# Expert weights in a ring of four 4 MB slots instead of six 2 MB slots, in a one-core decoder-layer kernel

## What is computed

```python
def moe_ffn(u, w_router, b_router, w_gate, b_gate, w_up, b_up, w_down, b_down):
    logits = (xf @ w_router + b_router).astype(F32)
    top_val, top_idx = lax.top_k(logits, TOP_K)
    gates = jax.nn.softmax(top_val, axis=-1)
    ...
        gt = jnp.minimum(xblk @ w_gate[e] + b_gate[e], SWIGLU_LIMIT)
        up = jnp.clip(xblk @ w_up[e] + b_up[e], -SWIGLU_LIMIT, SWIGLU_LIMIT)
        hdn = (up + 1.0) * gt * jax.nn.sigmoid(gt * SWIGLU_ALPHA)
        return hdn @ w_down[e] + b_down[e]
```

## Time and profile before

| | |
|---|---|
| runs | 1271.01, 1271.86, 1273.28 us, median 1271.86 |
| span of the profiled execution | 1267.4 us |
| profiled execution's own time beside its span | not listed apart from the runs; its span is 4.5 us under their median |
| busy | PE 1174.1 us, DVE 487.1 us, ACT 195.6 us, POOL 4.6 us |
| moved by DMA | 451.37 MB |

### The profile page before, as it was taken

One profiled execution on the slowest core, in us unless ns is written; L12 is line 12 of the kernel. 1 busy time (PEld: TensorE's weight loads), 2 busy tenths in 40 slices (PEclk: granted clock), 3 DMA queues, 4 the chain that ended last, 5 costly groups with the idle time before them and its releaser, 6 DMA issues.

```text
span 1267.4 us, 21244 instructions
## 1 busy us (share of the span) xinstructions
PE 1174.1 (93%) x8502; PEld 557.1 (44%) x8503; DVE 487.1 (38%) x1082; ACT 195.6 (15%) x431; POOL 4.6 (0%) x28
## 2 busy tenths in 40 slices
PE   8999989999998989999899999799999888879896
PEld 7888768874333333333333433233433333232333
DVE  2799998115342322232312233222232332323233
ACT  2143504022111100111101111100111110110112
POOL 0000000000000000000000000000000000000000
PEclk9999999999999999999989999999999999998998
DMA  9551329615999999899999899998999999999995
GB/s 395 208 186 67 142 105 330 268 53 209 411 428 425 427 429 400 329 430 427 428 430 402 342 430 428 428 428 353 392 430 430 429 427 429 428 430 428 428 429 228
DMA packets 36997, 451.37 MB, mean 356 GB/s; under 512 B 5112, under 2 KB 5656, under 8 KB 10080
## 3 DMA queue, kind: packets, MB, share of 16 engines
q1 hardware_dynamic: 35344, 449.02, 85.1%
q10 hardware_dynamic: 1616, 1.82, 0.4%
HBM read 443.57 MB, written 7.25 MB: 356 GB/s over the span
## 4 chain that ended last, share of the span: by engine, by line
PE 58%; DMA 28%; DVE 12%; issue 1%; DVEq 1%; ACT 0%; POOL 0%; SPq 0%; POOLq 0%; ACTq 0%
DMA ring<-in_w_experts 27%; PE ps L1467 25%; PE ps L1510 9%; DVE acts L724 5%; PE ps L1244 3%; PE ps L1346 3%; PE ps L1444 3%; PE ps L1519 2%; PE ps L1403 2%; PE ps L1477 2%; PE ps L1218 2%; DVE acts L819 1%; PE ps L1457 1%; PE ps L1337 1%; PE ps L1500 1%
## 5 line engine op out<-in xcount | busy, mean ns | idle before, releaser
L1467 PE MATMUL ps<-ring,extra 128*64 128x512 f32 x1824 | 424.1, 610 | 12.4 <-DMA ring<-in_w_experts 12.4
L1077 DVE TENSOR_TENSOR acts<-ps,acts 128x528 f32<-128x528 f32 x128 | 90.6, 708 | 403.0 <-PE ps L1477 201.6
L1467 PEld LDWEIGHTS ps<-ring,extra 128*64 128x64 f32 x1824 | 124.2, 139 | 265.5 <-issue 237.5
L1510 PE MATMUL ps<-ring,extra 128*32 128x256 f32 x3072 | 201.7, 398 | 38.3 <-DMA ring<-in_w_experts 34.8
L1510 PEld LDWEIGHTS ps<-ring,extra 128*32 128x32 f32 x3072 | 89.7, 113 | 140.0 <-DMA ring<-in_w_experts 50.9
L724 DVE SCALAR_TENSOR_TENSOR acts<-acts,small 128x256 f32<-128x256 f32 x224 | 91.3, 477 | 0.7 <-ACT acts L453 0.7
L1244 PE MATMUL ps<-acts,ring 128*128 128x280 f32 (+1 forms) x320 | 75.3, 394 | 0.3 <-ACT ring L524 0.3
L1244 PEld LDWEIGHTS ps<-acts,ring 128*128 128x128 f32 x320 | 60.5, 190 | 14.2 <-issue 1.0
L1244 PE MATMUL ps<-acts,extra 128*128 128x280 f32 x256 | 63.1, 409 | 1.9 <-DVE acts L706 1.9
L1091 DVE TENSOR_SCALAR extra<-ps 128x512 f32<-128x512 f32 x32 | 22.0, 689 | 96.3 <-PE ps L1467 81.0
L604 ACT ACTIVATE extra<-extra 128x512 f32<-128x512 f32 x32 | 19.7, 630 | 240.2 <-DVE extra L1082 240.2
(11 more groups left out here) (294 smaller groups left out, 898.9 us busy)
## 6 DMA issues: line engine op xcount, KB each, us to landing
ring<-in_w_experts SPq DMA_DIRECT2D x192, 2048.0 KB, 21.7
ring<-in_w_in_t SPq DMA_DIRECT2D x5, 2048.0 KB, 20.7
extra<-in_w_in_t SPq DMA_DIRECT2D x4, 2048.0 KB, 11.2
extra<-in_w_out_t SPq DMA_DIRECT2D x4, 1024.0 KB, 5.8
ring<-in_w_out_t SPq DMA_DIRECT2D x4, 1024.0 KB, 5.9
ring<-in_state_t SPq DMA_DIRECT2D x8, 512.0 KB, 6.9
ring<-dtx_rows SPq DMA_DIRECT2D x8, 512.0 KB, 5.8
out_ssm_s_t<-ring SPq DMA_DIRECT2D x8, 512.0 KB, 4.7
```

What stands on the lines that cost most here:

```text
L1077: TT(both, ps[:, 6:8, 0:TN], both, ALU.add).then_inc(ev["acc_done"], 1)
L1467: hs.append(MM(dst, src[:, o:o + HALF], piece(p)[:, k, 512 * h_:512 * (h_ + 1)], start=(fresh and kk == 0), stop=(kk == KT - 1), skip_grou ...
L1510: hs.append(MM(dst, src[:, o:o + QUAR], piece(p)[:, k, 256 * q:256 * (q + 1)], start=(fresh and kk == 0), stop=(kk == KT - 1), skip_group_ ...
```

## The change

Six things are changed together.

- The ring grows to 16 MB, four slots of one 4 MB matrix. Matrix m of the expert at place i lies in slot (3i + m) mod 4, so the slots turn with the experts, and each pair is asked for when the matrix four before it is used up, not three.
- To make room, `acts` shrinks from 16400 to 12064 columns: `cbuf`, `csmp` and `csq` move to the ring's fourth slot, the routing tables to `small`, and the scratch reserved per partition is set to 1024 bytes.
- Expert 1 always stands at place 1, and is treated as big. Its pairs 0 and 1 are loaded in the mixer, behind the state load of sample 7; its pairs 2 to 5 need no order.
- The places follow a new formula: places 0, 1, 4, 6, 8, ..., 30 are big, the others small. With the given counts the two-block experts stand at places 12, 18 and 24. Sixteen experts are big and sixteen small, as before.
- All four parts of the scatter stand behind the first gate piece. They alternate between banks 6 and 7 and banks 4 and 5, so part m waits for the add of part m-2. `find_order` stands behind the first scatter; the small expert's gate is written once and only its scatter branches on the width.
- TensorE's loop body is four experts (684 matmuls in the program instead of 398), seven turns after experts 0 to 3. The other engines keep loops of two experts.

```diff
-        ring = sb("ring", NP * PIECE)
+        MAT = 4 * PIECE
+        NQ = 4
+        ring = sb("ring", NQ * MAT)
...
-        acts = sb("acts", 16400)
+        acts = sb("acts", 12064)
...
+        cbuf = view(ring, 24576, KT, PAD + TP)
+        csmp = view(ring, 26864, KT, NB, CW)
...
+        csq = view(ring, 28848, KT, TN)
...
-        landed = [sem(f"pair_landed{i}") for i in range(NP // 2)]
+        landed = [[sem(f"pair_landed{par}_{i}") for i in range(NP // 2)] for par in range(2)]
...
+        def matrix_at(i, m):
+
+            return (i * 3 + m) % NQ * MAT
...
+        def pair_row(i, q):
+            return span(matrix_at(i, q // 2) + (q % 2) * 2 * PIECE, 2 * PIECE)
+
+        BACK_BANK = (6, 4, 6, 4)
...
+                if b == NB - NST_IN:
+                    sp.wait_ge(ev["var_mm"], 1)
+                    sp.wait_ge(ev["kept_out"], 64)
+                    prefetch(0, 1)
+                    prefetch(1, 1)
...
+            def stream(i, e, par, first=0):
+                for q in range(first, NP // 2):
+                    if q < 2:
+                        sp.wait_ge(ev["piece_used"], i * 8 - 16 + 6 + 2 * q)
+                    elif q < 4:
+                        sp.wait_ge(ev[("gate_half", "gate_used")[q - 2]], i)
+                    else:
+                        sp.wait_ge(ev["piece_used"], i * 8 - 8 + 2 * (q - 3))
+                    sp.dma_start(pair_row(i, q), expert_pair(e, q)).then_inc(landed[par][q], 16)
+
+            stream(1, 1, 1, 2)
             sp.wait_ge(ev["order_ready"], 1)
-            with sp.Fori(0, NE - 1) as i:
...
+            with sp.Fori(0, NE // 2 - 1) as ii:
+                for par in range(2):
+                    e = sp.value_load(order[0:1, bass.ds(ii * 2 + 3 + par, 1)], min_val=0, max_val=NE - 1)
+                    stream(ii * 2 + 2 + par, e, par)
...
-                    TT(both, ps[:, 6:8, 0:TN], both, ALU.add).then_inc(ev["acc_done"], 1)
+                    TT(both, ps[:, BACK_BANK[m]:BACK_BANK[m] + 2, 0:TN], both, ALU.add).then_inc(ev["acc_done"], 1)
...
             def scatter(n, m, n4):
-                if m:
-                    pe.wait_ge(ev["acc_done"], n4 + m)
+                if m > 1:
+                    pe.wait_ge(ev["acc_done"], n4 + m - 1)
...
+            def small_back(i):
+                former_ready(i)
+                for m in range(4):
+                    scatter_s(m, i * 4)
...
+            with pe.Fori(0, NE // 4 - 1) as t:
+                counts = [count_of(t * 4 + 5 + 2 * h) for h in range(3)]
+                for h in range(2):
+                    i = t * 4 + 4 + 2 * h
+                    big_expert(i, weights_of(2 * h, 0, t * 32 + 48 + 16 * h), counts[h], lambda: small_back(i), None)
+                    small_expert(i + 1, weights_of(2 * h + 1, 1, t * 32 + 48 + 16 * h), lambda: big_back(i + 1, counts[h]), counts[h + 1])
...
-    nc = _bacc.Bacc("TRN2", target_bir_lowering=False, num_devices=1)
+    nc = _bacc.Bacc("TRN2", target_bir_lowering=False, num_devices=1, dynamic_dma_scratch_size=1024)
```

More of the change, by code:

```diff
@@ new lines, in build, with rt @@
+        Pm = view(acts, 5984, 2, TN)
+        gp = view(acts, 6512, TN)
+        eq = view(acts, 7712, 3, TOPK, NE)
+        yo = view(acts, 7712, KT, TN)
+        fsq = view(acts, 2240, KT, TN)
+        frstd = view(acts, 5600, TN)
+        ro = [route0]
+        def rt(*dims):
+            n = 1
+            for d in dims:
+                n *= d
+            v = view(small, ro[0], *dims)
+            ro[0] += n
+            return v
+        slotp, gates, logit, top8 = rt(3, NE + 2), rt(3, NE + 2), rt(3, NE), rt(3, 8)
@@ L1036, in _ @@
             TT(wrap_a, wrap_a, wrap_b, ALU.add)
+            TT(place, place, fix16, ALU.add)
             v.drain()
-            STT(place, wrap_a, 2.0, place, ALU.mult, ALU.add)
+            TT(place, wrap_a, place, ALU.add)
             v.drain()
@@ L1437, in halves, with gather @@
                 return [ps[HALF * h:HALF * (h + 1), bank, :] for h in range(2)]
-            def gather(n):
+            def gather(n, release=False):
                 for b in range(n):
```

379 lines of the change are left out of this document (204 added, 175 removed).

## The result

| | before | changed |
|---|---|---|
| median of the runs on one chip | 1272.57 us (1271.01 to 1275.13) | 1315.17 us (1312.75 to 1316.99) |
| ratio | 1 | 1.0339 [1.0319, 1.0359] |
| span of the profiled execution | 1267.4 us | 1315.2 us |
| longest wait of PE | 2.8 us | 12.1 us |

The change makes the kernel 42.6 us slower. 1240 was predicted, with 1231 to 1260 as the range and 0.04 for slower. The added term of 4.5 us between span and median was wrong too: the profiled execution of the changed kernel took 1316.99 us, 1.8 above its span.

What follows compares the result with a forecast made beforehand. DMA and TensorE limit the expert stage in turns. DMA alone gave a 1231.6 us span; TensorE's 635.0 + 531.6 + 49.4 - 5.2 + 11.1 = 1221.9, plus 13.7, gave 1235.6, and plus 4.5, 1240 us; range 1231 to 1260.

Steps and rivals of the forecast that it cites:

- The added term of 4.5 us: End of the sum: the median of the runs lies 4.5 us above the profiled span, so this is added.
- the fifth term of TensorE's sum: TensorE's loop: five entries into a new turn of the long body, 2.22 us each, + 11.1 us.
- The rival that was nearest: TensorE's long loop body: each turn also pays for jumps inside it, 3.5 us, 1257 us; chance 0.16.
- The slower rival: Waits for issue at the 12 width branches of a turn, 2.22 us each, 1373 us; chance 0.04.
- The dips (b): DMA's three slow stretches at the two-block experts, 26.0 us in sum, filled by the longer ring.
- the early loads (a): Two 2 MB loads move from the expert stage to the mixer, saving 9.8 us of DMA time.
- The early stretch: Start of the expert stage, 308 to 340 us: DMA at 365 GB/s, 4.7 us short, left unchanged.
- TensorE's groups of six: Three groups of six places from place 12 on, each with one two-block expert: 177.2 us each, 531.6 in all.
- Place 12: First two-block expert's place in the new order: its start moves from 654.25 to 635.0 us.
- The scatter: Parts 2 and 3 wait for earlier adds: about 0.3 us per expert, 1.8 us per six places.
- The seven waits: Sign at the head of TensorE's loop: seven waits of PE for issue, near 2 us each.
- more than 27 blocks: Sign on the instruction queue: more than 27 instruction blocks if code is fetched again in the loop.

Runs made afterwards that it cites:

- The written-out kernel: The changed kernel with TensorE's loop written out as seven copies of the four experts, no backward branch; 1261.04 us, ratio 0.9929 to the kernel before.
- the light loads: The changed kernel with expert weights from place 1's third pair on loaded to a quarter of their columns; 1262.49 us.

## Why the prediction was wrong

**The failed step** is the fifth term of TensorE's sum, the entries into a new turn: "I take 2.22, because the new body is 1.7 times as long and a return to its head is a far jump". Measured 11.29 to 12.09 us, and 2.2 more at the lower clock: 14 in place of 2.22. Neither end of that bound came from a row that had the thing in it. Before's returns never left resident code, and its 2.22 was a wait after a jump forward. The edge was passed, and what lies behind it is not a higher price for the same thing but another regime: the body fetched again in every turn, with TensorE idle at the head for one fetch or two. The written-out kernel takes the term away, and the time with it.

In the span it adds up so. The prediction's loop cost 1235.6 - 1231.6 = 4.0 us above DMA's floor; measured it cost 1315.2 - 1255.2 = 60.0. The other 23.6 us of the 79.6 between forecast and result lie on DMA's side, below. The term also counts five entries, since the return at place 8 was to fall into DMA's slack.

The signs that the prediction had named for being wrong came. In the changed kernel the first two groups of six took 196.6 us each on the mean, against a limit of 185, and all three dips were over 5 us. Place 0 moved too, if little: it started at 303.53 us instead of 301.44.

**The rival that was nearest** was the code that is fetched inside each turn, with 0.16, at 3.5 us per turn. It asked the right question, whether the code stays, and I priced it from first-pass waits, where no jump back occurs. The slower rival put its waits at 12 branches and asked for 6.9 us per turn. That threshold was passed, but by one wait at the loop's head, where I had a term of 2.22, not at the branches. Their own share is small: L1562 waits 10.4 us in the whole run.

**The dips (b) and the early loads (a)** were right in direction and too large in size. In the written-out kernel the dips are 6.6 + 1.4 + 2.8 = 10.8 us (381, 418 and 408 GB/s), not 0. The early stretch, which I said would not change, ran at 306 GB/s from 300 to 360 us where before has 337, 4.3 us lost: the first request of the stream came 3.0 us later, after an order that is worked out behind the first scatter. The steady rate was 425 to 427 in most slices, where the prediction took 428; over 400 MB that is about 3 us. These 18 us are most of the 23.6 between DMA's predicted floor, 1231.6, and this span, 1255.2; about 5 are not accounted for. (a) and (b) promised 35.8 us; against the kernel before, written out too, 24 came, with the places and the scatter in them. How they divide was not tried.

**TensorE's groups of six** were right: 180.3, 180.3 and 174.2 us in the written-out kernel, against 177.2, with waits for weights of 0.0, 0.0 and 1.6 us in them. **Place 12** started at 646.1 instead of 635.0. So 11 of the 23.6 us were lost ahead of the first two-block expert, and of them the early stretch explains 4.3 and the steady rate about one; the rest is the part that is not accounted for. Places 30 and 31 took 60 us and not 49.4, since weights were late there: DMA was still the limit at the end.

**The scatter** was right: 26 waits of 0.37 us, 9.6 us in all, released by the add, 0.34 per expert. The mixer was nearly right: place 0 starts 2.1 us later than before, 1.1 in the written-out kernel, and whether the moved loads did that was not tried. **The seven waits** at the head were right in number, and **more than 27 blocks** was the sign that I had named for the right cause; it came, with 121. The added 4.5 us from span to median was no real term: every profiled execution whose own time is known read 1.8 to 1.9 us above its span, so that of the kernel before must have been a fast one.

## What to carry to other kernels

A loop body has a size up to which it is free and past which each turn pays. Before lengthening one, count its instructions as the engine sees them (a float32 matmul is four), code that never runs included, and look at the instruction queue: the resident loop here fetched its blocks once. In this kernel 1663 instructions stayed and some 1930 didn't. Past the edge there are two ways, a shorter body or straight code, and the second also pays: here 13 us, in the kernel before, whose short loop was free. A bound that comes from inside one regime says nothing about the other; where a change may cross such an edge, the case behind it needs a price of its own.

## What the runs showed that was not expected

- Padding that is never executed, 60 float32 matmuls, made the kernel 134 us slower. In waits for issue, 95.1 us stand at the returns and 43.8 inside the body, in twelve waits shortly behind the jump over the two-block code.
- The place of the code in memory matters: 128 instructions of shift changed each return from 11.3 to 12.1 us to 7.1 to 7.5, and the time from 1315.2 to 1301.0 by one run.
- One block of code takes some 6 us to come while weights stream at 424 GB/s or more (5.5 to 6.0 us from one start to the next in a return; 11.5 us for a wait with two, 6.5 to 7.5 for one), and some 3.5 us with the light loads.
- Straight code hides its fetches nearly wholly, but for those behind a forward jump: 7.8 us at the line after the skipped code. The 2.9 us at `bias`, six waits of 0.5 where token counts are loaded, may be something else; no row tells.
- After a return TensorE's granted clock was 0.50, the level of 1.2 GHz, in the four kernels where I read it (the changed one, its shifted and its light form, and the old one with four experts per turn), for 3 us and more; ahead of it the engine had stood idle for 6.5 us or longer.
